# Two-block transformer kernel with eight experts: PE's expert loop aligned to a 256-instruction block, and each expert unit transferred in two halves

## The chip, the cores and the metric

The kernel runs on one core of a Trainium2 chip. The metric is the device time of one execution in microseconds; lower is better. A core has five engines that run their own instruction streams and meet at semaphores: TensorE (PE, matmuls; its weight loads are shown as PEld), VectorE (DVE), ScalarE (ACT), GpSimd (POOL) and SyncE (SP), which here does nothing but issue DMA transfers. All data is float32.

## The reference

Two models run one after the other on 256 tokens of width 1024: a first block of two layers (attention and a gated recurrence, conv FFN), then a second block of two layers (pooling, mLSTM and forgetting attention mixers), the first with a dense SwiGLU and the second with a mixture of experts. The mixture is what this case is about. Each token picks its top 2 of 8 experts, and each expert is a SwiGLU of width 3584:

```python
def moe_swiglu(h, w_router, b_router, w_gate, w_up, w_down):
    logits = (t @ w_router).astype(jnp.float32) + b_router.astype(jnp.float32)
    top_v, top_e = lax.top_k(logits, TOP_K)
    gate = jax.nn.softmax(top_v, axis=-1)
    ...
    def one(args):
        xb, e = args
        return (jax.nn.silu(xb @ w_gate[e]) * (xb @ w_up[e])) @ w_down[e]
```

The result of each expert is added to the tokens that chose it, weighted by their gates, and a final norm follows.

## The kernel before

All weights of all layers are cut into *units* of at most 1 MB, 128 partitions by up to 2048 floats, and go through a ring of four slots in SBUF (`ring`, `NSLOT = 4`, `SLOT = 2048`). SP issues the transfers in the order in which PE uses the units. Ahead of each it waits until `unit_done`, which PE increments once at the end of each unit, says that the unit four places earlier has been used. PE waits for `slot{i}_full` of the slot, 16 increments a transfer. `lin_free` counts the PSUM banks that ACT or DVE have emptied.

The mixture is the last stage. DVE and ACT build selection matrices; PE gathers the tokens of an expert into `XG`, up to `CAP = 96` columns. An expert with more tokens than that is *dense*: it runs over all 256 tokens. Which branch is taken is read from `many` at run time, on each engine. With these inputs one expert of the eight is dense, the seventh.

PE's program for the mixture is a loop over the eight experts (`pe.Fori(0, N_EXPERTS)`, L875). Its body, in the order of the instructions:

- L880: two transposes of the selection weights, then waits for DVE's additions of the expert before (`mo_sc`) and for ACT's copy of the gathered tokens (`mo_xg`), a value load of the dense flag (L884) and a branch (L885)
- dense: one matmul for the gates (L888) and `up(e, H, T)`; sparse: `up(e, XG, CAP)`. `up` is a loop of 7 turns (L844) over 4 units (L854 issues its matmuls); a unit is a gate tile and an up tile, each of 8 matmul calls over k, or 16 in a sparse expert, whose columns are split into two strips of 64. The waits are at L851 and its neighbours.
- the gather of the next expert's tokens (L869)
- a second branch on the dense flag (L898), then `down`: a loop of 4 turns (L859) over 4 units of 896 KB, two to a tile, in `down_tile` (waits at L512 to L520, matmuls at L524), 14 matmul calls a unit, or 28 in a sparse expert
- sparse: 8 transposes (L911) and 8 matmuls that scatter the result to the tokens (L920), whose sums DVE adds to `X` (L1809)

The loop head of each engine is wherever the code ahead of it ends. An up unit in DRAM has its columns in the order (k, gate or up tile, column), so both tiles need the whole unit. SP's own loop over the experts has one wait and one `dma_start` a unit (L414 for the up units). ACT waits for `unit_done` ahead of each pair of up tiles and of each down tile, DVE ahead of the down tiles of a dense expert. `down_tile` is also used by the three feed-forward layers ahead of the mixture.

Of the kernel before, what the change touches and what calls it, by code (L numbers as in the profile page):

```python
# [6 lines left out]
P = 128  # L7
# [67 lines left out]
def build(nc, dram, out):  # L75
# [10 lines left out]
    MOE0 = base["moe_up"]  # L86
    PER_E = ET + 16

    ctx = ExitStack()
    with ctx:  # L90
# [56 lines left out]

        slot_full = [S(f"slot{i}_full") for i in range(NSLOT)]
        unit_done = S("unit_done")
        lin_free = S("lin_free")  # L150
# [31 lines left out]
        def slot_of(u):  # L182
            return u % NSLOT
# [187 lines left out]
        def _(sp):  # L371
            sp.dma_start(fst[:, :], dram["first"]).then_inc(S("first_in"), 16)

            def stream(name, u0, n, src):
# [15 lines left out]
                for j in range(loops * NSLOT, n):  # L390
                    one(j, 0)

            for name, n, w in STAGES:
                src = dram["proj0" if name.startswith("proj0_") else "mod_b" if name.startswith("mod_p") else name]
# [4 lines left out]
                elif name == "mod_b":  # L399
                    stream(name, base[name], n, src[MOD_P:])  # L400
                elif name == "mod_a":
                    for u in range(NSLOT):
                        sp.dma_start(ring[:, u, 0:w], src[u]).then_inc(slot_full[u], 16)
                    sp.dma_start(flat(X[:, :, :]), dram["xT"]).then_inc(S("x_in"), 16)
                    stream(name, NSLOT, n - NSLOT, src[NSLOT:n])
                    sp.dma_start(cst[:, :], dram["consts"]).then_inc(S("consts_in"), 16)
                    sp.dma_start(par[:, :], dram["params"]).then_inc(S("params_in"), 16)
                elif name == "moe_up":
                    with sp.Fori(0, N_EXPERTS) as e:
                        with sp.Fori(0, ET // NSLOT) as it:  # L410
                            for j in range(NSLOT):
                                u = MOE0 + j
                                sp.wait_ge(unit_done, e * PER_E + it * NSLOT + (u - NSLOT + 1))
                                sp.dma_start(ring[:, slot_of(u), :], src[e * ET + it * NSLOT + j])\  # L414
                                  .then_inc(slot_full[slot_of(u)], 16)
                        with sp.Fori(0, 16 // NSLOT) as it:
                            for j in range(NSLOT):
                                u = MOE0 + ET + j
                                sp.wait_ge(unit_done, e * PER_E + it * NSLOT + (u - NSLOT + 1))
                                sp.dma_start(ring[:, slot_of(u), 0:EDOWN_W], dram["moe_down"][e * 16 + it * NSLOT + j])\  # L420
                                  .then_inc(slot_full[slot_of(u)], 16)
                elif name != "moe_down":
                    stream(name, base[name], n, src)
# [6 lines left out]
        def _(pe):  # L430
# [35 lines left out]

            def fm_unit(u, tile, src, width, it=0, tiles_per_it=0, k_n=KT, ready=None, mod=None):

                w = unit(u, it).rearrange("p (k n) -> p k n", n=2 * P)
                for t in range(2):  # L470
# [7 lines left out]
                    if t == 0 and mod is not None:  # L478
                        mod_step(mod)
                mm.then_inc(unit_done, 1)  # L480

# [9 lines left out]

            def wout(name, src, width, ready=None):
                for j in range(4):
                    fm_unit(base[name] + j, tile_base[name] + 2 * j, src, width, ready=ready if j == 0 else None)

# [13 lines left out]
            def down_tile(u, tile, bank, src, width, half, it=0, e_units=0, units_it=NSLOT, tiles_it=NSLOT // 2, e=None, e_tiles=0, late=None):  # L509
# [3 lines left out]
                for s in range(2):  # L513
# [312 lines left out]
            def moe():  # L826
# [16 lines left out]
                def up(e, src, n):  # L843
                    with pe.Fori(0, ET // NSLOT) as it:  # L844
                        for j in range(NSLOT):
                            u = MOE0 + j
                            pe.wait_ge(slot_full[slot_of(u)], e * (16 * PER_E // NSLOT) + it * 16 + 16 * (u // NSLOT + 1))
                            w = ring[:, slot_of(u), :].rearrange("p (k n) -> p k n", n=2 * P)
                            for t in range(2):

                                pe.wait_ge(lin_free, e * per_t + it * (2 * NSLOT) + (t0 + 2 * j + t + 1))  # L851
                                for k in range(KT):
                                    for lo, m in strips(n):
                                        mm = pe.matmul(B[(t0 + 2 * j + t) % 4][lo:lo + m, 0:n], w[:, k, t * P + lo:t * P + lo + m],  # L854
                                                       src[:, k, 0:n], start=k == 0, stop=k == KT - 1)
                            mm.then_inc(unit_done, 1)

# [117 lines left out]
            for l in range(DEPTH):  # L975
# [16 lines left out]
                branch(l)  # L992
                wout(f"twout{l}", H[:, :, T:TC], T, ("merged", 8 * l, 1))
                norm(9 + 2 * l, T)
# [10 lines left out]
        def _(act):  # L1005
# [184 lines left out]
            def swiglu(name, width, e=None):  # L1190
                u0, t0 = base[name], tile_base[name]
                eu = 0 if e is None else e * PER_E
# [136 lines left out]
            with act.Fori(0, N_EXPERTS) as e:  # L1329
# [8 lines left out]
                with act.Else():  # L1338
                    with act.Fori(0, 16 // NSLOT) as it:
                        for j in range(NSLOT // 2):  # L1340
                            act.wait_ge(unit_done, it * NSLOT + (MOE0 + ET + 2 * j + 2) + e * PER_E)
                            dst = OG[:, bass.ds(it * (NSLOT // 2) + j, 1), :].rearrange("p a t -> p (a t)")
# [11 lines left out]
        def _(dve):  # L1354
# [313 lines left out]
            def add_down(u0, e=None):  # L1668

                eu = 0 if e is None else e * PER_E  # L1670
                with dve.Fori(0, 16 // NSLOT) as it:
                    for j in range(NSLOT // 2):
                        dve.wait_ge(unit_done, it * NSLOT + (u0 + 2 * j + 2) + eu)
                        x = X[:, bass.ds(it * (NSLOT // 2) + j, 1), 0:T].rearrange("p a t -> p (a t)")
# [79 lines left out]
            for l in range(DEPTH):  # L1754
# [8 lines left out]
                for k in range(KT):  # L1763
                    add_out(name, tile_base[name], k, (tile_base[name] + k) % 4, base[name] + k // 2 + 1)
                plain_norm(9 + 2 * l, W(f"ffn_g{l}", KT), H, S(f"norm{9 + 2 * l}_out"))
# [150 lines left out]
def layout(x):  # L1916
# [117 lines left out]
```

## Time and profile before

| | us |
|---|---|
| median of 3 runs | 3733.32 (3727.51 to 3740.18) |
| the profiled execution | 3727.8 |
| its span | 3726.0 |

| engine | busy us | share |
|---|---|---|
| PE | 3473.1 | 93% |
| PEld | 2716.8 | 73% |
| DVE | 679.7 | 18% |
| ACT | 661.4 | 18% |
| POOL | 128.8 | 3% |

The mixture runs from about 2473 us to 3712 us of the span. "Idle before" is the time that an engine stood still ahead of an instruction, and "<-" names what ended it; "issue" means that nothing which the profile shows was waited for. Matmul ends are modelled. The page cuts the span into 40 slices of 93 us; a digit is the busy share of a slice in tenths. The granted clock of TensorE has two levels, 1.2 and 2.4 GHz, shown as 0.5 and 1.0.

### The profile page before, as it was taken

How to read it: one execution, taken by the hardware profiler on the slowest of the kernel's cores; microseconds unless marked ns; L12 is line 12 of the kernel's file. 1: busy time of each engine (PE TensorE's matmuls, PEld its weight loads, DVE VectorE, ACT ScalarE, POOL GpSimd, SP SyncE). 2: the span in 40 equal slices, each digit the busy share in tenths (PEclk: the TensorE clock that was granted, in tenths of full speed). 3: DMA queues.
4: the chain of work that ended last, by engine and by line, in shares of the span. 5: the costliest groups of instructions: out<-in, count | busy, mean ns of one | idle time of the engine just before them, and what ended most of it. 6: DMA issues, size and time to landing. Idle time of an engine off the chain costs nothing.

```text
span 3726.0 us, 74216 instructions
## 1 busy us (share of the span) xinstructions
PE 3473.1 (93%) x32010; PEld 2716.8 (73%) x32011; DVE 679.7 (18%) x1582; ACT 661.4 (18%) x1422; POOL 128.8 (3%) x173
## 2 busy tenths in 40 slices
PE   7999789999999899999999999979998999999988
PEld 3456634444357688787888887779988988988888
DVE  1214622220012321213210114220000010011001
ACT  2214122210112431212110112111111111110001
POOL 0000010000000110200000000000000000000000
PEclk9999699999999999999999999989999999999999
DMA  6436012221223243342343443348887988944467
GB/s 251 179 147 227 3 45 79 79 68 62 84 85 102 91 148 135 119 140 101 127 144 135 141 143 108 119 159 349 332 331 301 370 330 309 368 148 153 138 237 270
DMA packets 94822, 638.60 MB, mean 171 GB/s; under 512 B 10784, under 2 KB 11824, under 8 KB 38592
## 3 DMA queue, kind: packets, MB, share of 16 engines
q1 hardware_dynamic: 92048, 627.58, 45.8%
q0 software_dynamic: 2608, 8.49, 0.7%
q8 instruction: 142, 2.33, 0.3%
q14 instruction: 24, 0.20, 0.0%
HBM read 634.98 MB, written 1.05 MB: 171 GB/s over the span
## 4 chain that ended last, share of the span: by engine, by line
PE 90%; DVE 4%; issue 3%; ACT 2%; DMA 1%; POOL 0%; SPq 0%; ACTq 0%; DVEq 0%; POOLq 0%
PE bank L476 31%; PE bank L854 20%; PE bank L524 17%; PE bank L544 5%; PE bank L488 4%; PE bank L811 2%; PE bank L440 2%; PE bank L450 1%; PE bank L869 1%; PE bank L580 1%; PE bank L562 1%; PE bank L569 1%; DVE RT L1359 1%; DVE Y L1376 1%; PE bank L920 1%
## 5 line engine op out<-in xcount | busy, mean ns | idle before, releaser
L476 PE MATMUL bank<-H,ring 128*128 128x256 f32 (+1 forms) x3744 | 1078.0, 450 | 25.3 <-ACT H L1024 22.2
L476 PEld LDWEIGHTS bank<-H,ring 128*128 128x128 f32 x3744 | 715.2, 192 | 373.2 <-issue 300.7
L524 PE MATMUL bank<-PROJ,ring 128*64 128x96 f32 (+2 forms) x7776 | 667.3, 282 | 15.7 <-ACT SC L1058 8.7
L524 PEld LDWEIGHTS bank<-PROJ,ring 128*64 128x64 f32 (+1 forms) x7776 | 547.6, 148 | 135.0 <-issue 103.1
L854 PE MATMUL bank<-MIX,ring 128*64 128x96 f32 x12544 | 539.0, 250 | 31.4 <-issue 31.2
L854 PEld LDWEIGHTS bank<-MIX,ring 128*64 128x64 f32 x12544 | 535.2, 140 | 36.3 <-issue 36.3
L854 PE MATMUL bank<-H,ring 128*128 128x256 f32 x896 | 196.6, 383 | 0.0
L1689 DVE TENSOR_TENSOR PROJ<-SC,bank 128x96 f32 (+2 forms) x246 | 70.9, 288 | 664.2 <-ACT SC L1199 660.1
L854 PEld LDWEIGHTS bank<-H,ring 128*128 128x128 f32 x896 | 172.3, 192 | 24.6 <-issue 0.6
L544 PE MATMUL bank<-H,ring 128*128 128x256 f32 x768 | 178.5, 390 | 3.9 <-ACT PROJ L1080 3.7
L544 PEld LDWEIGHTS bank<-H,ring 128*128 128x128 f32 x768 | 148.3, 196 | 28.2 <-issue 7.4
L1557 DVE SCALAR_TENSOR_TENSOR SC<-bank,par,SC 128x510 f32<-128x510 f32 (+1 forms) x176 | 100.2, 611 | 358.8 <-ACT SC L1053 352.9
L1199 ACT ACTIVATE SC<-bank 128x96 f32<-128x96 f32 (+1 forms) x246 | 68.2, 277 | 520.3 <-PE bank L854 415.2
L488 PE MATMUL bank<-ring,H 128*128 128x256 f32 x704 | 157.5, 386 | 2.8 <-ACT PROJ L1028 1.7
L488 PEld LDWEIGHTS bank<-ring,H 128*128 128x128 f32 x704 | 135.5, 193 | 24.5 <-issue 5.8
L1199 ACT ACT_TABLE_LOAD x61 | 78.3, 1283 | 410.7 <-PE bank L854 373.2
L440 PE MATMUL bank<-H,cst 128*128 128x256 f32 (+1 forms) x208 | 81.0, 543 | 36.0 <-ACT H L1012 33.9
L1359 DVE RECIPROCAL RT<-RT 128x256 f32<-128x256 f32 (+1 forms) x13 | 30.8, 2368 | 382.7 <-ACT RT L1016 382.7
L440 PEld LDWEIGHTS bank<-H,cst 128*128 128x128 f32 x208 | 41.4, 218 | 74.4 <-ACT H L1012 60.2
L811 PE MATMUL bank<-MIX,ring 128*128 128x256 f32 x384 | 83.4, 380 | 3.3 <-ACT MIX L1302 3.3
L1053 ACT ACTIVATE SC<-bank,par 128x512 f32<-128x512 f32 (+1 forms) x88 | 54.2, 666 | 175.0 <-PE bank L476 174.9
L476 PE MATMUL bank<-MIX,ring 128*128 128x512 f32 (+1 forms) x256 | 83.1, 486 | 1.2 <-DVE MIX L1541 0.8
(276 smaller groups left out, 2004.5 us busy)
## 6 DMA issues: line engine op xcount, KB each, us to landing
ring<-in_moe_up SPq DMA_DIRECT2D x224, 1024.0 KB, 5.9
ring<-in_moe_down SPq DMA_DIRECT2D x128, 896.0 KB, 5.9
ring<-in_up SPq DMA_DIRECT2D x44, 1024.0 KB, 4.8
ring<-in_mod_b SPq DMA_DIRECT2D x40, 1024.0 KB, 5.0
ring<-in_tproj SPq DMA_DIRECT2D x32, 1024.0 KB, 4.8
ring<-in_proj SPq DMA_DIRECT2D x26, 1024.0 KB, 4.8
ring<-in_gates SPq DMA_DIRECT2D x24, 1024.0 KB, 4.8
ring<-in_down SPq DMA_DIRECT2D x32, 704.0 KB, 4.0
```

Of the source, the lines that this page charges most:

```text
L440: mm = pe.matmul(B[4][:, 0:width], mean_d, H[:, k, 0:width], start=k == 0, stop=k == KT - 1)
L476: mm = pe.matmul(B[(tile + t) % 4][:, 0:width], w[:, k, t * P:(t + 1) * P], src[:, k, 0:width], start=k == 0, stop=k == k_n - 1)
L488: mm = pe.matmul(B[(tile + t) % 4][:, 0:2 * P], H[:, k, t * P:(t + 1) * P], w[:, k, :], start=k == 0, stop=k == KT - 1)
L524: mm = pe.matmul(B[bank][lo:lo + m, 0:width], w[:, k, lo:lo + m], src(s * half + k), start=s == 0 and k == 0, stop=s == 1 and k == half - 1)
L544: mm = pe.matmul(gate_bank(i)[:, 0:T], w[:, k, (i % 2) * P:(i % 2 + 1) * P], H[:, k, 0:T], start=k == 0, stop=k == KT - 1)
L811: mm = pe.matmul(B[tile % 4][:, 0:T], w[:, b, k, :], src(k), start=k == 0, stop=k == 3)
L854: mm = pe.matmul(B[(t0 + 2 * j + t) % 4][lo:lo + m, 0:n], w[:, k, t * P + lo:t * P + lo + m], src[:, k, 0:n], start=k == 0, stop=k == KT - 1)
L1053: mm = act.activation(CONV[:, j % 2, t, 0:width], B[(t0 + 2 * j + t) % 4][:, 0:width], ACT.Identity, bias=col(3), scale=col(1))
L1199: act.activation(CONV[:, j % 2, 0, 0:width], B[(t0 + 2 * j) % 4][:, 0:width], ACT.Silu).then_inc(S("sw_s"), 1)
L1359: step(dve.reciprocal(RT[:, 0:width], RT[:, 0:width]))
L1557: ins = dve.scalar_tensor_tensor(out=o, in0=u, scalar=col, in1=o, op0=ALU.mult, op1=ALU.add)
L1689: dve.tensor_tensor(PROJ[:, bass.ds(it * (NSLOT * width) + j * width, width)], g, B[(t0 + 2 * j + 1) % 4][:, 0:width], ALU.mult)\
```

## The change

Two things, and what they need around them.

Each expert unit goes as two transfers of half the width. For the up units the order in DRAM becomes (tile, k, column), so the first half holds the gate tile and the second the up tile; for the down units a half holds 7 of the 14 k steps. Both halves go to the same slot: the first signals `slot{i}_full`, the second a new semaphore `slot{i}_half`. PE increments `unit_done` after each half and waits for the second half's semaphore ahead of it, and SP issues a half as soon as that half of the slot is free. So that the counts fit, the four units of `twout1` count double, and the waits of ACT and DVE in the experts are rewritten.

```diff
+    HALVES0 = base["twout1"] + 8
...
+            def half_units(e, it, j, src, width):
+
+                for h, full in ((0, slot_full), (1, slot_half)):
+                    s = slot_of(MOE0 + j)
+                    sp.wait_ge(unit_done, e * (2 * PER_E) + it * (2 * NSLOT) + (HALVES0 + 2 * (j - NSLOT) + h + 1))
+                    sp.dma_start(ring[:, s, h * (SLOT // 2):h * (SLOT // 2) + width], src[:, h * width:(h + 1) * width])\
+                      .then_inc(full[s], 16)
...
                             for j in range(NSLOT):
-                                u = MOE0 + j
-                                sp.wait_ge(unit_done, e * PER_E + it * NSLOT + (u - NSLOT + 1))
-                                sp.dma_start(ring[:, slot_of(u), :], src[e * ET + it * NSLOT + j])\
-                                  .then_inc(slot_full[slot_of(u)], 16)
+                                half_units(e, it, j, src[e * ET + it * NSLOT + j], SLOT // 2)
...
-                    w = ring[:, slot_of(uu), 0:half * P].rearrange("p (k n) -> p k n", n=P)
-                    for k in range(half):
-                        for lo, m in strips(width):
-                            mm = pe.matmul(B[bank][lo:lo + m, 0:width], w[:, k, lo:lo + m], src(s * half + k),
-                                           start=s == 0 and k == 0, stop=s == 1 and k == half - 1)
-                    mm.then_inc(unit_done, 1)
+                    parts = 1 if e is None else 2
+                    for q in range(parts):
+                        n = half // parts
+                        if q == 1:
+                            pe.wait_ge(slot_half[slot_of(uu)], it * (units_it // NSLOT) * 16 + e * (16 * e_units // NSLOT) + 16 * ((uu - MOE0) // NSLOT + 1))
+                        w = ring[:, slot_of(uu), q * (SLOT // 2):q * (SLOT // 2) + n * P].rearrange("p (k n) -> p k n", n=P)
+                        for k in range(n):
+                            for lo, m in strips(width):
+                                mm = pe.matmul(B[bank][lo:lo + m, 0:width], w[:, k, lo:lo + m], src(s * half + q * n + k),
+                                               start=s == 0 and q == 0 and k == 0, stop=s == 1 and q == parts - 1 and k == n - 1)
+                        mm.then_inc(unit_done, 1)
...
-                            w = ring[:, slot_of(u), :].rearrange("p (k n) -> p k n", n=2 * P)
+                            w = ring[:, slot_of(u), :].rearrange("p (t k n) -> p t k n", t=2, n=P)
                             for t in range(2):
 
+                                if t == 1:
+                                    pe.wait_ge(slot_half[slot_of(u)], e * (16 * PER_E // NSLOT) + it * 16 + 16 * (j // NSLOT + 1))
                                 pe.wait_ge(lin_free, e * per_t + it * (2 * NSLOT) + (t0 + 2 * j + t + 1))
...
-                            mm.then_inc(unit_done, 1)
+                                mm.then_inc(unit_done, 1)
...
                 pe.wait_ge(S("mo_sel"), 1)
                 gather()
+                pe.addr_align(256)
                 with pe.Fori(0, N_EXPERTS) as e:
...
-                    act.wait_ge(unit_done, it * NSLOT + (u0 + j + 1) + eu)
+                    if e is None:
+                        act.wait_ge(unit_done, it * NSLOT + (u0 + j + 1))
+                    else:
+                        act.wait_ge(unit_done, it * (2 * NSLOT) + (HALVES0 + 2 * j + 2) + e * (2 * PER_E))
...
-    out["moe_up"] = np.concatenate([paired(f["moe_w_gate_2"][0][e], f["moe_w_up_2"][0][e]) for e in range(N_EXPERTS)])
+    up = np.concatenate([paired(f["moe_w_gate_2"][0][e], f["moe_w_up_2"][0][e]) for e in range(N_EXPERTS)])
+    out["moe_up"] = np.ascontiguousarray(up.reshape(-1, P, KT, 2, P).transpose(0, 1, 3, 2, 4)).reshape(-1, P, SLOT)
```

## Rows read from the trace of the kernel before

**Rows 1.** The page, part 2: busy tenths in 40 slices of the span.
```profile
PE   7999789999999899999999999979998999999988
...
DMA  6436012221223243342343443348887988944467
```

**Rows 2.** Waits from 2500 us: engine line <- releaser: us in total, times, longest.
```profile
PE bank L880 <- issue: 29.8, 7, 7.8
...
PE bank L854 <- issue: 26.7, 12, 3.3
...
PE bank L524 <- issue: 5.2, 7, 1.2
...
PE bank L869 <- issue: 2.1, 1, 2.1
...
PE bank L854 <- DMA ring<-in_moe_up: 0.2, 1, 0.2
```

**Rows 3.** Timeline of PE, second expert: start us, length, instruction, count [idle before].
```profile
2597.56 3.72 PE L920 MATMUL bank<-Y,H 96*128 96x256 f32 x16 [0.25 <-ACT H L1346]
2605.00 0.61 PE L880 MATMUL bank<-cst,Y 128*96 128x128 f32 x2 [3.72 <-issue]
2608.40 1.22 PE L854 MATMUL bank<-MIX,ring 128*64 128x96 f32 x10 [2.79 <-issue]
2611.02 75.85 PE L854 MATMUL bank<-MIX,ring 128*64 128x96 f32 x1782 [1.40 <-issue]
...
2691.60 37.58 PE L524 MATMUL bank<-PROJ,ring 128*64 128x96 f32 x896 [0.99 <-issue]
```

**Rows 4.** PE's sequencer by line: count, ns min/median/max, first and last start.
```profile
L844 PEldq COMPARE_BRANCH  x56: 76/208/232, 2490.0 to 3661.6; - x56
...
L875 PEldq COMPARE_BRANCH  x8: 76/6428/6825, 2598.2 to 3707.1; - x8
...
L884 PEldq TENSOR_LOAD <-many x8: 298/310/503, 2474.8 to 3580.4; - x8
...
L885 PEldq COMPARE_BRANCH  x9: 78/1810/3292, 2475.7 to 3581.1; - x9
...
L885 PEldq COMPARE_BRANCH  x1: 366/366/366, 2475.7 to 2475.7; - x1
...
L898 PEldq COMPARE_BRANCH  x9: 81/2411/4208, 2556.0 to 3664.2; - x9
...
L520 PEldq EVENT_SEMAPHORE  x32: 51/51/51, 2563.0 to 3700.1; - x32
```

**Rows 5.** DMA queues: second expert (2604.9 to 2737.5 us), then 2621 to 2688 us.
```profile
q1 hardware_dynamic: 6337, 44.04, 85.5%
q8 instruction: 9, 0.15, 0.5%
...
q1 hardware_dynamic: 3658, 26.32, 100.1%
...
ring<-in_moe_up SPq DMA_DIRECT2D x22, 1024.0 KB, 5.7
```

**Rows 6.** The page, part 5: sparse up matmuls, count | busy us, mean ns | idle before.
```profile
L854 PE MATMUL bank<-MIX,ring 128*64 128x96 f32 x12544 | 539.0, 250 | 31.4 <-issue 31.2
```

**Rows 7.** Windows: stretch, length, busy us of PE, PEld, DVE, ACT, POOL, PEclk, DMA share, GB/s.
```profile
2605.00:2615.20 10.20, 6.01 (x64) 5.30 (x66) 1.26 (x5) 0.00 (x0) 0.00 (x0) 0.50 0.02 5
2621.10:2684.40 63.30, 63.30 (x1542) 63.30 (x1537) 6.10 (x24) 13.64 (x31) 0.00 (x0) 1.00 1.00 393
```

**Rows 8.** Timeline of DVE: its second addition behind the first expert.
```profile
2599.59 0.69 DVE L1809 TENSOR_TENSOR X<-X,bank 128x512 f32<-128x512 f32 x1 [0.18 <-PE bank L920]
```

**Rows 9.** SP's issue of an up unit: ns min/median/max.
```profile
L414 SPq DMA_DIRECT2D ring<-in_moe_up x224: 332/333/343, 2413.9 to 3652.2; - x112
```

**Rows 10.** DMA queues: 3300 to 3400 us (8 KB rows), 1215 to 1245 us (bias, 4 KB rows on q0).
```profile
q1 hardware_dynamic: 2020, 14.70, 41.9%
...
q0 software_dynamic: 800, 2.62, 27.4%
```

More of the change, by code:

```diff
@@ L148, in build @@
         slot_full = [S(f"slot{i}_full") for i in range(NSLOT)]
+        slot_half = [S(f"slot{i}_half") for i in range(NSLOT)]
         unit_done = S("unit_done")
@@ L411, in _ @@
                             for j in range(NSLOT):
-                                u = MOE0 + j
-                                sp.wait_ge(unit_done, e * PER_E + it * NSLOT + (u - NSLOT + 1))
-                                sp.dma_start(ring[:, slot_of(u), :], src[e * ET + it * NSLOT + j])\
-                                  .then_inc(slot_full[slot_of(u)], 16)
+                                half_units(e, it, j, src[e * ET + it * NSLOT + j], SLOT // 2)
                         with sp.Fori(0, 16 // NSLOT) as it:
                             for j in range(NSLOT):
[L418 to L421, printed above, removed]
+                                half_units(e, it, ET + j, dram["moe_down"][e * 16 + it * NSLOT + j], EDOWN_W // 2)
                 elif name != "moe_down":
@@ L465, in mod_step, with fm_unit @@
                     mod_turn(n - 1)
-            def fm_unit(u, tile, src, width, it=0, tiles_per_it=0, k_n=KT, ready=None, mod=None):
+            def fm_unit(u, tile, src, width, it=0, tiles_per_it=0, k_n=KT, ready=None, mod=None, inc=1):
                 w = unit(u, it).rearrange("p (k n) -> p k n", n=2 * P)
@@ L479, in fm_unit @@
                         mod_step(mod)
-                mm.then_inc(unit_done, 1)
+                mm.then_inc(unit_done, inc)
             def tm_unit(u, tile, tts):
@@ L490, in tm_unit, with wout @@
                 mm.then_inc(unit_done, 1)
-            def wout(name, src, width, ready=None):
+            def wout(name, src, width, ready=None, inc=1):
                 for j in range(4):
-                    fm_unit(base[name] + j, tile_base[name] + 2 * j, src, width, ready=ready if j == 0 else None)
+                    fm_unit(base[name] + j, tile_base[name] + 2 * j, src, width, ready=ready if j == 0 else None, inc=inc)
             def pairs(name, width, ready):
@@ L853, in up @@
                                     for lo, m in strips(n):
-                                        mm = pe.matmul(B[(t0 + 2 * j + t) % 4][lo:lo + m, 0:n], w[:, k, t * P + lo:t * P + lo + m],
+                                        mm = pe.matmul(B[(t0 + 2 * j + t) % 4][lo:lo + m, 0:n], w[:, t, k, lo:lo + m],
                                                        src[:, k, 0:n], start=k == 0, stop=k == KT - 1)
-                            mm.then_inc(unit_done, 1)
+                                mm.then_inc(unit_done, 1)
                 def down(e, hidden, n):
@@ L992, in _ @@
                 branch(l)
-                wout(f"twout{l}", H[:, :, T:TC], T, ("merged", 8 * l, 1))
+                wout(f"twout{l}", H[:, :, T:TC], T, ("merged", 8 * l, 1), inc=1 + l)
                 norm(9 + 2 * l, T)
@@ L1191, in swiglu @@
                 u0, t0 = base[name], tile_base[name]
-                eu = 0 if e is None else e * PER_E
                 et = 0 if e is None else e * (2 * ET + KT)
@@ L1340, in _ @@
                         for j in range(NSLOT // 2):
-                            act.wait_ge(unit_done, it * NSLOT + (MOE0 + ET + 2 * j + 2) + e * PER_E)
+                            act.wait_ge(unit_done, it * (2 * NSLOT) + (HALVES0 + 2 * ET + 4 * j + 4) + e * (2 * PER_E))
                             dst = OG[:, bass.ds(it * (NSLOT // 2) + j, 1), :].rearrange("p a t -> p (a t)")
@@ L1668, in add_down @@
             def add_down(u0, e=None):
-                eu = 0 if e is None else e * PER_E
                 with dve.Fori(0, 16 // NSLOT) as it:
                     for j in range(NSLOT // 2):
-                        dve.wait_ge(unit_done, it * NSLOT + (u0 + 2 * j + 2) + eu)
+                        if e is None:
+                            dve.wait_ge(unit_done, it * NSLOT + (u0 + 2 * j + 2))
+                        else:
+                            dve.wait_ge(unit_done, it * (2 * NSLOT) + (HALVES0 + 2 * ET + 4 * j + 4) + e * (2 * PER_E))
                         x = X[:, bass.ds(it * (NSLOT // 2) + j, 1), 0:T].rearrange("p a t -> p (a t)")
@@ L1763, in _ @@
                 for k in range(KT):
-                    add_out(name, tile_base[name], k, (tile_base[name] + k) % 4, base[name] + k // 2 + 1)
+                    add_out(name, tile_base[name], k, (tile_base[name] + k) % 4, base[name] + (1 + l) * (k // 2 + 1))
                 plain_norm(9 + 2 * l, W(f"ffn_g{l}", KT), H, S(f"norm{9 + 2 * l}_out"))
```

## The prediction

> **What bounds the kernel now.** The page first: PE's line is 8 or 9 through the last third, where the DMA line is 8 and 9 too, but for the dense expert's 4 [rows 1]. That third is the loop over the eight experts: 1,252 of 3,726 us. So I ask two things of it: what PE idles for, and how near the DMA queue is to its limit.
>
> The waits of PE from 2500 us on name almost only "issue": 29.8 us ahead of L880 (the loop's head), 26.7 ahead of L854 (the up tiles), 5.2 ahead of L524 (the down tiles), 2.1 ahead of L869; the longest wait for a transfer is 0.2 us [rows 2]. The timeline of one expert shows the pattern: after the last matmul of L920, 3.72 us of nothing, then two transposes, 2.79 us, ten matmuls, 1.40 us, and then 1,782 matmuls without a break; 0.99 us more ahead of the down tiles [rows 3]. All seven sparse experts look like this, the first without the gap at its head.
>
> What these gaps are, the sequencer's rows tell. A branch that closes an inner loop takes 0.21 us (L844). The branch that closes the expert loop (L875) takes 6.43 us, the one into the sparse half of the first If (L885) 1.81 us (0.37 us in the first expert, where its target had come in by straight code), the one of the second If (L898) 2.41 [rows 4]. And in the same stretches the instruction queue moves packets: 9 in one expert, each 16 KB, which is 256 instructions of 64 bytes; none from 2621 to 2688 us, where the up loop turns around six times [rows 5]. So PE waits for its own code.
>
> **Why nine.** A matmul call in f32 is two weight loads and two matmuls, four instructions (12,544 records for 7 x 28 x 2 x 8 x 2 calls) [rows 6]; a transpose is two. From the source, one body of the expert loop has 256 + 512 (up dense, sparse), 64 (gather), 224 + 448 (down), 4 + 4 + 16 + 32 for L880, L888, L911 and L920, and 64 waits, register steps and branches in the compiled program: 1,624 instructions. The 1.40 us stop comes after ten matmuls, that is at instruction 312 of the body, in every expert [rows 3]; a block border lies there, so the head sits 56 instructions ahead of a border. The body then touches 8 blocks, and PE fetches one block ahead: 9, as counted. Aligned to the border it touches 7 (1,624 plus at most some 30 for the new waits, under 1,792), with the one ahead 8.
>
> **The change, part by part.**
> *Alignment.* It pays if PE keeps 8 blocks. The trace bounds what is kept: the up loop (520 instructions, three blocks, a fourth ahead) turns with no packet, so at least 4; with 9 in use every one is fetched anew, so at most 8 [rows 5]. I take 8, the upper end; the lower one is a rival. The Trainium skill (Runtime: NRT & Kernel Launch, "Instruction fetch mechanics") gives PE's instruction memory as 128 KiB, 2,048 instructions in blocks of 256, which is eight, and by it the misses would end; a note in the same section speaks of only two lines, and that the trace contradicts, since the up loop spans three.
>
> What then goes: idle 29.8 + 26.7 + 5.2 + 2.1 = 63.8 us [rows 2]. With it the slow clock: PE is granted 0.50 for 10.2 us after each head gap (its 1.2 GHz level), 1.00 in the loops [rows 7]. At full clock L854 takes 63.30 / 1542 = 41.05 ns a record, so 12,544 would take 514.9 us; they took 539.0 [rows 6, 7]: 24.1 us, 3.4 an expert, 20.7 for the six that follow a back edge. The dense expert starts the same way, 3 us. Together 87.5 us.
>
> What stays: the head still runs wait, value load, branch. DVE's second add ends at 2600.28 us [rows 8], from there the value load needs 0.31 and the branch 0.37 us [rows 4], and the register steps about them, down to the first wait of the up loop, as much again, 1.4 us in all, while PE is busy until 2601.28 and then 0.6 us with L880: 0 to 1 us late, I take 0.5, six times 3.0. After the dense expert no S matmuls cover it: 2.5 us, and perhaps a short slow clock, 1.5. The first expert visits every block for the first time: its 0.8 us at L524 stays, and the sparse entry now lies in the second block, which comes in only once the head is reached (1 to 3 us), and 56 padding slots run once, beside the gather's queue (0 to 1): 2.5. Sum 10.3, leaving 77 us.
>
> *Halves.* No wait for a unit is worth removing (0.2 us the longest), so the earlier release gives nothing by itself; it adds room, since 7 halves (3.5 MB) can be under way behind the one in use where it was 3 units. Costs: PE gets one more wait per unit, 44 an expert; L520's takes 0.05 us of the sequencer, twice that with a register step [rows 4], up to 4 us an expert, under a queue that PE is working off without a break: 0, and up to 4 if the sequencer were not ahead. SP issues twice as often: 0.33 us each plus 0.2 for wait and registers [rows 9], 1.1 us in the 2.64 us of a unit (64 records x 41.05 ns), hidden; behind it on SP stands only the next unit.
>
> The transfers are what can bite. In one expert the queue takes 85.5% of 132.6 us, 113.4 us [rows 5]; rows of 8 KB become 4 KB. Lone 8 KB rows moved 14.70 MB in 100 us at 41.9% (351 GB/s at full share), the lone 4 KB rows of GpSimd's bias queue 2.62 MB in 30 us at 27.4% (319): 10% dearer [rows 10]; against the full loop's 393 GB/s [rows 7] they are 23% dearer. The near end is 0. I take 5%, midway to 10, because the lone rows meet an idle queue and these do not: 119 us of transfers in an expert that PE then needs 132.6 - 8.9 (idle) - 3.4 (clock) + 0.5 = 120.8 us for. Covered, barely; 1 us of waits an expert, 7 in all. The Trainium skill (DMA: Bandwidth & Descriptors, "Measured") speaks against this part: it asks for DMAs of at least 1 MiB to reach 75% of the peak. The trace does not bear it out where several are under way: a 1 MB unit takes 5.7 us to land [rows 5], yet one is consumed each 2.64. By that page's rule the halves would cost and not be hidden; that is the transfer rival below, priced from rows.
>
> Sum: 77 - 7 = 70 us. The profiled execution took 3727.8 us (span 3726.0), so 3657.8; the median shown is 5.5 above it: 3663 us.
>
> **The rivals.**
> *Fewer than eight blocks kept* (10%). For it: nothing in the trace shows more than four. Then every block is still fetched, but better placed: the border after ten matmuls is gone (1.40 us; the next comes 224 instructions later, 4.6 us, more than the 3.2 us between the resumptions at 2608 and 2611 [rows 3]), the down tiles' block is in (0.99), and the back edge no longer queues behind the fetch ahead (about 1): 3.5 us x 7, 25 us, 3708.
> *Transfers take over* (10%). The misses end but 4 KB rows cost the full 10%: 124.7 us an expert plus a us of waits, 4.9 above 120.8, seven times: 34 us back, 3733 - 43 = 3690.
> *Slower* (6%). The same mechanism at the far price: 23% dearer rows make 139.5 us of transfers, 6.9 above today's 132.6, times seven, 48 us, less 15 kept at the dense expert: 3766. It decides from 132.6 / 113.4, 17% dearer on. Against it: nothing under way in the loops is a lone transfer.
> *No effect* (6%): the misses stay as long as they are, or the new waits eat it: 3733.
>
> **How the numbers follow.** 68% for the forecast (3640 to 3685 by its own terms), and the rest as above. The range 3638 to 3708 holds the forecast, the transfer case and the edge of the fewer-blocks case. A measurement of this kernel tells about 0.3% (11 us) from nothing. Faster 68 + 10 + 10 = 88%, same 6%, slower 6%.
>
> **What would show it.** Packets of the instruction queue in an expert: none from the second on, where there are 9 [rows 5]; L875's branch near 0.2 to 0.4 us; L880 with no 3.7 us gap, clock 1.00 from the second expert on; L854 near 515 us + the first expert's loss. A sparse expert of 120 to 122 us. Wrong if the packets stay at 9 an expert, or if the waits at L854 and L524 now name the transfers for more than 2 us an expert.

## The result, and the profile after

The changed kernel takes 3646.86 us, the median of 4 runs (3644.37 to 3648.53), the kernel before 3735.69 us beside it (3727.51 to 3740.18): a ratio of 0.9764, 95% interval 0.9745 to 0.9783. That is 88.8 us less where 70 were forecast. The profiled execution has a span of 3642.6 us, 83.4 less than the one of before. The profiled execution of before lay 8 us under the median of its kernel, the one after 2.5 us, which is the rest.

The page of the changed kernel (parts 2, 3 and 5). Its lines have moved: L865 is the old L854, L892 the old L880, L880 the old L869, L533 the old L524, L932 the old L920, and the loop of L875 is now L887.

```profile
PEclk9999699999999999999999999988999999999999
DMA  6446011211221433333244433237999999954477
...
q1 hardware_dynamic: 142736, 627.61, 47.5%
...
q8 instruction: 79, 1.29, 0.1%
...
L865 PE MATMUL bank<-MIX,ring 128*64 128x96 f32 x12544 | 522.6, 247 | 10.0 <-issue 10.0
```

The instruction queue q8 moved 142 packets in all in the kernel before and 79 now. In the experts' third of the span the DMA row has risen from 8 and 9 to 9, and the granted clock shows nothing below 0.9 there but for the 8 of the slice from 2459 to 2550 us, in which the first expert begins. The sparse up matmuls are busy 522.6 us where it was 539.0, with 10.0 us of idle time ahead of them where it was 31.4 [rows 6].

The waits of PE from 2500 us to the end: engine, line <- releaser: us in total, times, longest.

```profile
PE bank L865 <- issue: 5.0, 6, 2.0
PE bank L932 <- ACT H L1360: 1.7, 7, 0.2
PE bank L444 <- ACT H L1024: 1.2, 1, 1.2
PE bank L900 <- DVE Y L1807: 1.0, 1, 1.0
```

This is the whole list. The 63.8 us of "issue" [rows 2] are 5.0, and no line names a transfer. The timeline of PE in the first, second and last expert (start us, length, instruction, count, idle before):

```profile
2467.39 5.55 PE L880 MATMUL bank<-Y,MIX 128*128 128x96 f32 x32 [2.49 <-DVE Y L1800]
2474.95 0.64 PE L892 MATMUL bank<-cst,Y 128*96 128x128 f32 x2 [2.01 <-issue]
2480.68 76.10 PE L865 MATMUL bank<-MIX,ring 128*64 128x96 f32 x1792 [5.09 <-issue]
...
2598.97 3.72 PE L932 MATMUL bank<-Y,H 96*128 96x256 f32 x16 [0.24 <-ACT H L1360]
2602.53 0.38 PE L892 MATMUL bank<-cst,Y 128*96 128x128 f32 x2
2603.52 74.14 PE L865 MATMUL bank<-MIX,ring 128*64 128x96 f32 x1792 [0.61 <-issue]
...
2681.33 37.29 PE L533 MATMUL bank<-PROJ,ring 128*64 128x96 f32 x896
...
2723.44 0.38 PE L892 MATMUL bank<-cst,Y 128*96 128x128 f32 x2
```

```profile
3505.10 75.79 PE L865 MATMUL bank<-MIX,ring 128*64 128x96 f32 x1792 [1.97 <-issue]
```

Against [rows 3]: the gap at the head (3.72) is gone, the 2.79 ahead of the up tiles is 0.61, the stop after ten matmuls (1.40) and the one ahead of the down tiles (0.99) are gone. From one head to the next it is 120.91 us (2723.44 - 2602.53) where it was 132.6 [rows 5]. What the sequencer and the clock did, by PE's sequencer rows (count, ns min/median/max, first and last start), by two windows of the second expert that answer to [rows 7], the second of which runs 4 us into the gather, and by the DMA queue of that expert (packets, MB, share):

```profile
L887 PEldq COMPARE_BRANCH  x8: 67/209/209, 2599.6 to 3623.7; - x8
```

```profile
L886 PEldq NOP  x57: 13/13/13, 2470.5 to 2474.6; - x57
```

```profile
2602.50:2612.70 10.20, 9.59 (x225) 9.31 (x225) 2.67 (x10) 2.03 (x4) 0.00 (x0) 1.00 0.69 218
2618.60:2681.90 63.30, 63.30 (x1478) 63.09 (x1476) 6.11 (x24) 12.67 (x31) 0.00 (x0) 1.00 1.00 392
```

```profile
q1 hardware_dynamic: 12726, 44.23, 95.9%
```

The branch that closes the expert loop took 6.43 us [rows 4] and takes 0.21. The granted clock behind this head is 1.00 in place of 0.50. The instruction queue has no row in this expert. The 57 padding instructions (L886) start over 4.1 us, one every 73 ns.

### The profile page after: what moved, and what is told of

Its sections match the earlier page's. It is cut to its first block, busy times and chain, and to the rows that moved or that the text cites. A ratio compares the mean times of both kernels' runs of the same rounds, so it can differ in the third digit from the quotient of the medians.

```text
span 3642.6 us, 75769 instructions
## 1 busy us (share of the span) xinstructions
PE 3446.0 (95%) x32010; PEld 2696.9 (74%) x32011; DVE 679.6 (19%) x1582; ACT 661.5 (18%) x1422; POOL 128.8 (4%) x173
## 3 DMA queue, kind: packets, MB, share of 16 engines
q0 software_dynamic: 2608, 8.49, 0.7%
## 4 chain that ended last, share of the span: by engine, by line
PE 92%; DVE 4%; ACT 2%; issue 1%; DMA 1%; POOL 0%; SPq 0%; DVEq 0%; ACTq 0%; POOLq 0%
PE bank L480 32%; PE bank L865 20%; PE bank L533 18%; PE bank L553 5%; PE bank L492 4%; PE bank L820 2%; PE bank L444 2%; PE bank L454 1%; PE bank L589 1%; PE bank L880 1%; PE bank L571 1%; PE bank L578 1%; DVE RT L1373 1%; DVE Y L1390 1%; PE bank L932 1%
## 5 line engine op out<-in xcount | busy, mean ns | idle before, releaser
L480 PE MATMUL bank<-H,ring 128*128 128x256 f32 (+1 forms) x3744 | 1076.8, 450 | 25.3 <-ACT H L1036 22.2
L533 PE MATMUL bank<-PROJ,ring 128*64 128x96 f32 (+2 forms) x7776 | 665.5, 282 | 9.8 <-ACT SC L1070 8.7
L533 PEld LDWEIGHTS bank<-PROJ,ring 128*64 128x64 f32 (+1 forms) x7776 | 547.0, 147 | 127.3 <-issue 96.5
L865 PE MATMUL bank<-MIX,ring 128*64 128x96 f32 x12544 | 522.6, 247 | 10.0 <-issue 10.0
L865 PEld LDWEIGHTS bank<-MIX,ring 128*64 128x64 f32 x12544 | 521.3, 138 | 12.0 <-issue 12.0
L865 PE MATMUL bank<-H,ring 128*128 128x256 f32 x896 | 193.7, 379 | 0.0
L865 PEld LDWEIGHTS bank<-H,ring 128*128 128x128 f32 x896 | 170.2, 190 | 23.4 <-issue 0.3
L820 PE MATMUL bank<-MIX,ring 128*128 128x256 f32 x384 | 83.4, 380 | 3.3 <-ACT MIX L1316 3.3
```

Of the source, the lines that this page charges most:

```text
L480: mm = pe.matmul(B[(tile + t) % 4][:, 0:width], w[:, k, t * P:(t + 1) * P], src[:, k, 0:width], start=k == 0, stop=k == k_n - 1)
L820: mm = pe.matmul(B[tile % 4][:, 0:T], w[:, b, k, :], src(k), start=k == 0, stop=k == 3)
```

## The experiments

The theory: PE keeps eight blocks of 256 instructions; the loop of before needed nine with the one that is fetched ahead, so that every block was fetched anew in each expert; all of the gain is the end of that, idle time and slow clock together, and the halves give nothing. The rivals: the halves carry part of it; fewer than eight blocks are kept and only their placing became better; the transfers are the next bound, close by; the slow clock is no consequence of the gaps.

**Alignment alone.** The kernel before with one line more:

```diff
+                pe.addr_align(256)
                 with pe.Fori(0, N_EXPERTS) as e:
```

> The kernel before with nothing but the alignment ahead of PE's loop over the experts; units stay whole (1 MB, rows of 8 KB). Theory (the gain is the instruction blocks that stay, the halves only add room): no instruction packets from the second expert on, L854's busy time near 520 us, and waits for transfers at the up and down tiles of 0 to 2 us an expert, since the slack of a whole unit was thin: 3647 to 3660 us. Rival (the halves carry part of the gain, since without them PE now meets its transfers): more than 3 us of waits for transfers an expert, 3670 us or more. Rival (the halves cost): below 3644 us.

Measured: 3649.59 us (3644.66 to 3653.95), ratio 0.9772 (0.9755 to 0.9788), span 3642.9. Its waits from 2500 us (L854 and L524 are the up and down tiles here):

```profile
PE bank L854 <- issue: 4.9, 6, 2.0
...
PE bank L524 <- DMA ring<-in_moe_down: 0.5, 2, 0.3
```

There are 79 instruction packets, as in the changed kernel, and the span is within 0.3 us of its span. The alignment carries all of the gain. A unit moved whole makes PE wait 0.5 us in all; that is what halves could save.

**Halves alone.** The changed kernel without that line:

```diff
-                pe.addr_align(256)
                 with pe.Fori(0, N_EXPERTS) as e:
```

> The changed kernel without the alignment: two halves a unit, the loop's head where the code ahead of it ends (56 instructions ahead of a block border, as before). Theory: nine instruction packets an expert as before, the gaps ahead of L892, L865 and L533 of 3.7, 2.8 + 1.4 and 1.0 us stay, the clock falls to 0.50 at each head, and the halves neither pay nor cost: 3730 to 3740 us. Rival (the halves bring part of the 89 us): 3720 us or less. The queue's time an expert, 113.4 us in whole units, is expected at 115 to 119 us.

Measured: 3734.52 us (3729.88 to 3739.29), ratio 0.9996 (0.9986 to 1.0005), 142 instruction packets. The instruction queue in its second expert, and PE's timeline of that expert's start:

```profile
q8 instruction: 9, 0.15, 0.4%
```

```profile
2603.78 3.72 PE L931 MATMUL bank<-Y,H 96*128 96x256 f32 x16 [0.25 <-ACT H L1359]
2611.19 0.39 PE L891 MATMUL bank<-cst,Y 128*96 128x128 f32 x2 [3.69 <-issue]
2614.89 1.06 PE L865 MATMUL bank<-MIX,ring 128*64 128x96 f32 x9 [3.30 <-issue]
2617.77 75.78 PE L865 MATMUL bank<-MIX,ring 128*64 128x96 f32 x1783 [1.82 <-issue]
```

The gaps of before stand where they stood, the one ahead of the down tiles a little longer (1.63 us where it was 0.99). Twice the transfers, the added waits and half the row length cost nothing that can be measured.

**Where the head lies in its block.** Three kernels that differ from the changed one in one number, which says at which slot of a block the loop begins. The body has 1,629 instructions; with the one that stands between the padding and the loop's first, an offset of 152 puts it into 1,782 slots, seven blocks; 176 leaves 14 instructions for an eighth block, 184 leaves 22.

```diff
-                pe.addr_align(256)
+                pe.addr_align(256, offset=152)
```

> The changed kernel with the loop placed 152 instructions behind the border, not on it: its 1,629 instructions then end at slot 1,781 of 1,792, so they still touch seven blocks, while every branch target lies elsewhere in its block. Theory (what counts is that the blocks touched and the one fetched ahead are eight): no packets from the second expert on, 3644 to 3655 us, the padding (208 instructions run once) costing up to 6 us. Rival (what counts is a head or a target on a border): the gaps come back, 3700 us or more.

> As the run at 152, but 176 behind the border: the last few instructions of the body, the loop's branch among them, fall into an eighth block, and with the one ahead there are nine. Theory (PE keeps eight blocks and drops the oldest): all of them are fetched anew in each expert, nine packets each, and the time is back at that of before within 1%: 3715 to 3740 us. Rival (PE drops something else than the oldest, or keeps more than eight): one or two packets an expert or none, 3645 to 3680 us.

> The loop's head eight instructions further into its block than with offset 176, so that 22 of the body's instructions lie in an eighth block in place of 14. With 14 the sparse experts fetched no ninth block; with about 36, as the loop of before lay, they fetched nine blocks an expert. If the fetch ahead starts once the sequencer has come some 16 instructions into a block: nine packets an expert return, 3715 to 3740 us. If it needs more than 22: as with offset 176, ten packets in the last expert alone, 3666 us.

Offset 152: 3654.05 us (3653.73 to 3657.35), ratio 0.9783 (0.9766 to 0.9799), 80 packets. The one more comes at 3634 us, behind the loop. Nothing is missed in the loop, but the padding is longer. Its rows, and the first head on PE's timeline:

```profile
L886 PEldq NOP  x209: 13/13/13, 2472.9 to 2488.4; - x105
```

```profile
2469.86 7.11 PE L880 MATMUL bank<-Y,MIX 128*128 128x96 f32 x32 [2.48 <-DVE Y L1800]
2488.76 0.63 PE L892 MATMUL bank<-cst,Y 128*96 128x128 f32 x2 [11.78 <-issue]
2491.01 75.61 PE L865 MATMUL bank<-MIX,ring 128*64 128x96 f32 x1792 [1.62 <-issue]
```

209 instructions, 15.5 us, where the changed kernel has 57 and 4.1; PE stands 11.78 us ahead of L892 in place of 2.01, and gets 3.5 back at L865 (1.62 in place of 5.09). That is 6.3 us of idle time more, once; the median is 4.5 us above the one with alignment alone and 7.2 above the changed kernel's.

Offset 176: 3666.38 us (3662.92 to 3669.04), ratio 0.9814 (0.9797 to 0.983). I had expected nine packets an expert; this was wrong. The queues from 2620 to 3500 us, a stretch that the second to the seventh expert fill (they run from 2614 to 3516), and from 3500 us to the end (packets, MB, share), and PE's timeline of the last expert:

```profile
q1 hardware_dynamic: 75022, 260.58, 80.6%
```

```profile
q1 hardware_dynamic: 13412, 44.04, 73.0%
q8 instruction: 10, 0.16, 0.5%
```

```profile
3516.21 0.40 PE L892 MATMUL bank<-cst,Y 128*96 128x128 f32 x2 [2.00 <-issue]
3520.29 2.02 PE L865 MATMUL bank<-MIX,ring 128*64 128x96 f32 x21 [3.68 <-issue]
...
3604.81 37.27 PE L533 MATMUL bank<-PROJ,ring 128*64 128x96 f32 x896 [1.87 <-issue]
```

In the first stretch the instruction queue has no row at all, and a window up to 3511 us has none either: six experts run out of eight blocks without a packet, until the end of the sixth, the dense one. Then ten packets come with the last expert. So a loop that reaches 14 instructions into its eighth block keeps all eight, and a ninth block was fetched ahead only behind the dense expert. That expert gets to the loop's end by a jump into the eighth block, the sparse ones by straight code; that this is the reason no run shows. The span is 20 us longer than the changed kernel's, mostly by the padding (233 instructions, 17.2 us) and by these gaps of the last expert.

Offset 184: 3748.63 us (3743.46 to 3750.52), ratio 1.0027 (1.0012 to 1.0041). The queues of its second expert, and PE's timeline of it:

```profile
q8 instruction: 9, 0.15, 0.5%
```

```profile
2624.17 0.40 PE L892 MATMUL bank<-cst,Y 128*96 128x128 f32 x2 [3.96 <-issue]
2627.96 1.70 PE L865 MATMUL bank<-MIX,ring 128*64 128x96 f32 x17 [3.40 <-issue]
2630.90 75.35 PE L865 MATMUL bank<-MIX,ring 128*64 128x96 f32 x1775 [1.24 <-issue]
...
2711.98 38.93 PE L533 MATMUL bank<-PROJ,ring 128*64 128x96 f32 x896 [1.99 <-issue]
```

Nine packets an expert are back, and with them 10.6 us of gaps in each (3.96 + 3.40 + 1.24 + 1.99). Eight instructions of place are worth some 80 us (ratios of 1.0027 and 0.9814). That it is slower than the kernel before is for the most part its padding, 241 instructions in 17.7 us. Between 14 and 22 instructions in, the ninth block begins to be fetched; with nine in use all nine are lost each time round, with eight none. That is the count of eight kept, bounded from both sides. "Every one or none" is what happens if the block used longest ago is dropped, and also if the one fetched first is; no run tells these two apart. Fewer than eight kept is out. Why the step lies between 14 and 22 these runs don't show.

**The changed kernel once more**, beside the next three.

> The changed kernel once more, for comparison on the chip of the next three: 3647 us within 4, 0.5 us of idle time at most at a head from the second expert on.

3647.6 us (3644.01 to 3648.31), ratio 0.9769 (0.9755 to 0.9782). The idle time at the second head is 0.61 us again, a little over the 0.5 that I had allowed.

**What an idle time at the head costs.** Eleven loads more of the dense flag, at each head:

```diff
-                    dense = pe.value_load(many[0:1, bass.ds(e, 1)], min_val=0, max_val=1)
+                    for _ in range(12):
+                        dense = pe.value_load(many[0:1, bass.ds(e, 1)], min_val=0, max_val=1)
```

> The changed kernel with the load of the dense flag made twelve times in a row in place of once at each expert's head. PE is idle there, the code stays in its eight blocks and no transfer is touched: this puts back an idle time like the one removed, and nothing else. A load took 310 ns, so eleven more are 3.4 us an expert. If an idle time costs itself alone: 8 x 3.4 = 27 us, 3674 us. If, as my sum had it, the granted clock falls to half after each of them as it did after the gaps of before (10.2 us at 0.50, about 3 us each): 27 + 8 x 3 = 51 us, 3698 us, with 10.2 us at 0.50 behind every head and the L865 matmuls at 530 us or more busy in place of 522.6.

Measured: 3709.77 us (3706.45 to 3712.84), ratio 0.9938 (0.9923 to 0.9953); 79 instruction packets. The second expert on the timeline, and a window at its start:

```profile
2613.89 75.87 PE L865 MATMUL bank<-MIX,ring 128*64 128x96 f32 x1792 [7.67 <-issue]
```

```profile
2610.70:2617.50 6.80, 3.61 (x46) 3.62 (x48) 0.00 (x0) 0.00 (x0) 0.00 (x0) 0.50 0.00 0
```

A load costs 0.64 us with the two steps behind it, not the 0.31 of the load alone that I reckoned with, so the idle time is 7.67 in place of 0.61 us. It is about 7 us more at six heads, 6.2 at the dense expert's and 3.9 at the first, where PE stood still in any case (9.03 in place of 5.09). The clock falls to 0.50 here too, though no instruction is missing: for 6.8 us, 3.61 of them busy, and the up tiles take 75.87 in place of 74.14 us. By the waits of PE the idle time ahead of the up tiles grew by some 53 us over the eight experts, L865's busy time by 9.4 (522.6 to 532.0). So this idle time at the head brings the slow clock with it though its cause is another, and costs itself and 1.7 us; the 62 us measured (3709.77 against the 3647.6 beside it) are these two. With the loads taken at their real length, the first theory (idle alone) gives 56 and the second, at 3 us for each clock, 80: the slow clock is there, but it costs the up tiles 1.7 us here, where behind the gaps of before it cost them 2.9 (1.22 + 75.85 [rows 3] against 74.14).

**How much room the transfers have.** The halves with rows of 2 KB and then of 1 KB (1.75 and 0.88 KB for the down units), from DRAM laid out for it. This is the edit for 2 KB; for 1 KB it has `c=4` and `src[4 * h:4 * h + 4]`:

```diff
-                    sp.dma_start(ring[:, s, h * (SLOT // 2):h * (SLOT // 2) + width], src[:, h * width:(h + 1) * width])\
+                    sp.dma_start(ring[:, s, h * (SLOT // 2):h * (SLOT // 2) + width].rearrange("p (c w) -> p c w", c=2), src[2 * h:2 * h + 2].rearrange("c p w -> p c w"))\
```

> The changed kernel with each half of an expert's unit moved as rows of 2 KB (1.75 KB for down) in place of 4 KB (3.5 KB), from memory laid out for it: the same bytes in twice the packets. The queues were busy 0.96 of an expert's 120.9 us in after, 116 us. Rows of 4 KB in place of 8 KB cost 3.6% more queue time; if the price is a fixed one for each packet, about 12 ns, the next halving costs 7% more, 124 us of transfers an expert. My theory, that transfers then become the bound: a sparse expert takes 122 to 127 us, waits of PE for the ring's transfers appear, 3655 to 3690 us. Rival, that the queues have the room: 120.9 us an expert, no waits, 3647 us. Second rival, that small rows cost in proportion much more (20% or more): 140 us an expert, over 3770 us.

> The changed kernel with each half of an expert's unit moved as rows of 1 KB (0.88 KB for down). With rows of 2 KB no wait appeared, though the queues were busy 100.8% of an expert's 120.9 us. Packets of 8192, 4096 and 2048 bytes took 337, 174 and 91.5 ns on average, so one of 1024 bytes should take about 50.5 ns and the same bytes 10% more than with 2 KB: 134 us of transfers in an expert. My theory: now transfers are the bound, PE waits for the ring at L865 and L533, a sparse expert takes 130 to 136 us, the time is 3700 to 3750 us. Rival, that the busy shares overstate what the queues must do and there is room still: 121 us an expert, 3647 us.

2 KB: 3646.16 us (3643.11 to 3650.27), ratio 0.9768 (0.9753 to 0.9783): no change, against my theory. 1 KB: 3680.9 us (3679.82 to 3684.3), ratio 0.9851 (0.9836 to 0.9866): 34 us more. The queue in the second expert with 2 KB and then with 1 KB, and that expert's up tiles with 1 KB:

```profile
q1 hardware_dynamic: 23973, 44.12, 100.8%
```

```profile
q1 hardware_dynamic: 46713, 44.29, 108.4%
```

```profile
2611.86 78.88 PE L865 MATMUL bank<-MIX,ring 128*64 128x96 f32 x1792 [0.61 <-issue]
```

The waits of PE don't name the ring in this expert even with 1 KB; at a granted clock of 1.00 all the same, its up tiles are shown busy for longer (78.88 in place of 74.14 us). SP's waits tell who is late. SP waits for PE to free a half of a slot; first the changed kernel in its second expert, then the one with 1 KB:

```profile
SPq L400 <- PE bank L865: 44.9, 56, 6.5
SPq L400 <- PE bank L533: 20.6, 31, 4.1
```

```profile
SPq L400 <- PE bank L533: 17.6, 31, 2.8
SPq L400 <- PE bank L865: 16.5, 21, 4.4
```

The up tiles of an expert free 56 halves. In the changed kernel SP stood waiting for every one of them, 44.9 us of 74: the transfers are ahead of PE. With 1 KB it waited for 21, 16.5 us: in most of the up loop the transfers come last, and an expert takes 125.6 us (2611 to 2736). The bound is there, as I had it, but at a third of its price: 4.7 us an expert over PE's 120.9, where 134 us of transfers would have made it 13. So the packets' times, and with them the shares over 100%, overstate what a queue must do, and the real room of the changed kernel is larger than the 4% that its share (95.9% in that expert) leaves: from 116 us of packets' time in an expert (95.9% of 120.9) to 122 nothing was lost, and at 136 (108.4% of 125.6) 4.7 us.

**The padding out of the way.** Its 4.1 us are paid once, on PE's path. Two attempts, the alignment ahead of the first gather, and ahead of PE's wait for the router (6.2 us for DVE):

```diff
+                pe.addr_align(256)
                 pe.wait_ge(S("mo_sel"), 1)
                 gather()
-                pe.addr_align(256)
```

```diff
+                pe.addr_align(256, offset=135)
                 pe.wait_ge(S("rt_w"), 2)
...
-                pe.addr_align(256)
```

> The changed kernel with the alignment two statements earlier, ahead of the wait for the selection and of the first gather, so that the padding (56 instructions at 72 ns, 4 us) and the fetch of the first blocks run while PE waits for VectorE and ScalarE in any case; the loop's body is still seven blocks and a short part of the eighth. My theory, that the padding and the first fetch are paid on PE's path once: the idle times of 2.0 and 5.1 us in the first expert of after fall to the 2 to 3 us that ScalarE's gather copy and the code of the first expert cost, the span is 4 to 5 us shorter, 3642 us. Rival, that PE's path there is set by VectorE and the padding is hidden in after too: no difference within 1 us. Second rival, that the head's new place costs a block that has to be kept: nine instruction packets an expert come back, 3700 us or more.

> The changed kernel with the same alignment asked for 121 instructions earlier, ahead of PE's wait for the second half of the router (offset 135, so that the loop's head comes to lie at the same slot of its block as in the changed kernel). The padding is 57 instructions again, 4.1 us at 72 ns, but it now stands where PE waits 6.2 us for VectorE in any case (L832). My theory, that the padding is paid on PE's path once where it stands now and is free there: 2 to 4 us shorter than the changed kernel, 3644 us. In the first expert the idle time of 2.0 us goes, and the one of 4.6 to 5.1 us behind it stays or falls. Rival, that the idle times there come from fetching the loop's first blocks, which the padding only hides: no difference within 1 us, because the fetch takes the padding's place.

The first: 3651.49 us (3647.85 to 3652.3), ratio 0.9779 (0.9765 to 0.9792), 4 us worse than the changed kernel beside it and not better. What I had wrong is the count: 64 instructions earlier the border is the same one, so the padding is longer by as many. Its rows and the first head:

```profile
L884 PEldq NOP  x121: 13/13/13, 2471.1 to 2479.9; - x121
```

```profile
2479.96 6.95 PE L880 MATMUL bank<-Y,MIX 128*128 128x96 f32 x32 [9.88 <-issue]
...
2490.03 75.77 PE L865 MATMUL bank<-MIX,ring 128*64 128x96 f32 x1792 [2.90 <-issue]
```

The second, with an offset that brings the padding back to 57: 3647.37 us (3647.15 to 3649.53), ratio 0.9762 (0.9748 to 0.9775). On its timeline the 2.01 us at L892 are gone and 2.80 of the 5.09 at L866 (here the up tiles) stay:

```profile
2480.63 0.54 PE L892 MATMUL bank<-cst,Y 128*96 128x128 f32 x2
2483.97 75.80 PE L866 MATMUL bank<-MIX,ring 128*64 128x96 f32 x1792 [2.80 <-issue]
```

From the last matmul ahead of the first gather to the second head it is 3.2 us shorter than in the changed kernel run beside the first attempt (134.85 and 138.0 us). In the times this can't be told from nothing (0.9762 against 0.9769). No version beats the changed kernel by more than the measurement can tell.

## Why the prediction was right, and where it was off

- *PE waits for its own code, nine packets an expert; eight blocks are kept; aligned, the packets end.* Right, each part: 142 packets became 79, which is nine for each of the seven later experts, L875's branch fell from 6.43 to 0.21 us, and the offsets 176 and 184 bound the eight from both sides. It is as in the Trainium skill (Runtime: NRT & Kernel Launch, "Instruction fetch mechanics"), which gives PE 2,048 instructions. Its note of two lines, which it reckons from a memory of 32 KiB, does not hold for PE, since with offset 176 eight blocks were in use for six experts without a packet. That the head lay 56 instructions ahead of a border, read from the stop after ten matmuls, is confirmed by the 57 padding instructions: what is aligned is the one instruction that stands ahead of the loop's first.
- *The sum, on one footing.* PE's groups by line from the end of the router on, all of them: idle time 75.3 us before and 18.4 after, 56.9 less; busy time 24.3 less, of which the sparse up tiles 16.4 (539.0 to 522.6), the dense ones 2.9 (196.6 to 193.7), the gather 1.9, the down tiles 1.7 and the head's small matmuls 1.5. One of the groups after:

```profile
L533 PE MATMUL bank<-PROJ,ring 128*64 128x96 f32 (+1 forms) x6720 | 357.8, 255 | 0.0
```

- *Idle time: 63.8 less 8.8 that stays, 55.0.* It was 56.9. At five heads 0.61 us stays (0.5 forecast), behind the dense expert 1.97 (2.5). The first expert is right in sum and wrong in its parts: the padding was taken at 0 to 1 us and takes 4.1, of which the run with the padding out of the way got 3.2 back (2.01 and 5.09 us of idle time show ahead of L892 and L865), but the gap ahead of the down tiles, which the sum had kept, and the stop after ten matmuls went there too.
- *Slow clock: 23.7 less 1.5 that stays, 22.2.* It was 24.3, with two errors against each other, so that its nearness to the forecast is in part luck. The up tiles gave less than the sum had: at full clock an expert's take 74.14 us and not the 73.6 that 41.05 ns a record made, and the last one kept its slow start (75.79). The matmuls beside the gaps gave 5 us (gather, down tiles, head), and the sum had left them out.
- *Halves at nothing; waits for transfers, 7 us.* The first is right (0.9996, 0.9986 to 1.0005). The second is the term that was mis-sized, and most of the miss: it was 0. 4 KB rows took about half of the 5% more queue time that I took: 2.2% more in the second expert (95.9% of 120.9 us, 115.9 us, where it was 113.4), 2.9% by the mean packet of the stage (337 ns, and two of 173.5); the 3.6% that I reckoned with for the 2 KB rows was too much. And a queue time just under PE's time doesn't make waits here; not even 100.8% did. The rule of the Trainium skill (DMA: Bandwidth & Descriptors, "Measured") that asks for transfers of 1 MiB does not bear here, as [rows 5] had said: 512 KB ones are as good with several under way.
- *The end.* 70 us forecast, 83.4 in the spans: 7 of the 13 between are the transfers' term, 2.1 the clock's, 1.9 the idle time's; PE came to the stage 0.7 us earlier, and 1.5 are left over, which may be the overlap of the matmuls' modelled ends. The forecast of 3663 us set the median 5.5 us above the profiled execution; it lay 2.5 above it. All of these point the same way, to less time than was forecast, and none touches the mechanism.
- One reading of the prediction was wrong without bearing on its sum: the resumptions at 2608 and 2611 us are 2.6 us apart and not 3.2 [rows 3].
- The rivals: fewer blocks kept fell with offset 176. Transfers taking over at 10% dearer fell with the halves themselves, which were 2% dearer; 2 KB rows were 8% dearer than the whole units (122 us against 113.4) and still cost nothing. With 1 KB rows, 20% dearer (136 us), the mechanism comes true at a third of the price that these times would give. Slower, at 23% dearer, was never near.

## What to carry to other kernels

When a steady loop shows packets of the instruction queue and "issue" gaps at its head, count its instructions in blocks of 256, from where the head lies, and the one fetched ahead: here nine lost everything in every turn and eight nothing, so some 80 us hung on eight instructions of place. Alignment was then the whole cure, its padding was run once at some 73 ns an instruction, and growth of the body over the last border takes the gain back (22 instructions did, 14 did not). Whether transfers were late was to be read from what SP waited for, not from a queue's share.

## What the runs showed that was not expected

- A padding instruction is shown 13 ns long but one starts every 73 to 75 ns: 57 took 4.1 us, 121 took 8.8, 209 took 15.5.
- A loop that ends 14 instructions into its last block, reached by straight code, ran without the block behind it (offset 176); one that ends 22 in did not (offset 184). Behind the one expert that reaches it by a jump, 14 were enough to lose all eight.
- The clock was at 0.50 for 10.2 us behind a gap of 3.7 us, through those of 2.8 and 1.4 that follow [rows 3, 7], and for 6.8 us around the end of a single gap of 7.7 us (eleven loads): about the same idle time in one piece had the shorter slow stretch.
- A transfer queue busy 100.8% of the time by its packets cost PE nothing; at 108.4% it cost 4.7 us in 121, and PE's rows of that expert showed that as longer matmuls and not as a wait.
